# One 8 KB gather per expert slot from a side-by-side U and V table, and a weighted sum through diagonals

## What is computed

```python
s = jnp.einsum('thcd,ckd->thck', q, subkeys)         # q = xb @ wq
sv, si = lax.top_k(s, PEER_TOPK)
cand = sv[:, :, 0, :, None] + sv[:, :, 1, None, :]   # 16 x 16 sums
top_v, top_pos = lax.top_k(cand, PEER_TOPK)
eidx = jnp.take_along_axis(cidx, top_pos, axis=-1)
g = jax.nn.softmax(top_v)
u = u_tab[eidx]
a = jax.nn.gelu(jnp.einsum('td,thkd->thk', xb, u))
v = v_tab[eidx]
return jnp.einsum('thk,thkd->td', g * a, v)
```

## Time and profile before

| | us |
|---|---|
| median of 3 runs | 4904.78 (4903.73 to 4910.56) |
| the profiled execution, its own time | 4917.18 |
| the profiled execution, its span | 4915.5 |
| first gather of PEER issued at | 1783.13 |
| busy in the span: PE, DVE, POOL, ACT | 3810.6, 2952.9, 2278.9, 437.3 |
| moved by DMA | 1213.27 MB, of which 1124.21 MB by POOL's queue |

### The profile page before, as it was taken

How to read it: one execution, slowest core, us unless ns; L and a number is a source line. 1 busy time by engine, 2 the same in 40 slices (tenths; PEclk the granted TensorE clock), 3 DMA queues, 4 the chain that set the end, 5 groups by cost and what they waited for, 6 DMA issues and landing times.

```text
span 4915.5 us, 38276 instructions
## 1 busy us (share of the span) xinstructions
PE 3810.6 (78%) x11459; PEld 1541.3 (31%) x11459; DVE 2952.9 (60%) x7681; ACT 437.3 (9%) x1045; POOL 2278.9 (46%) x2121
## 2 busy tenths in 40 slices
PE   5699899899999853157777777767777777777789
PEld 3355355355445432112222222222222222211122
DVE  4466656646656658866666666656666656666620
ACT  2112112112212200000000000000000000000000
POOL 0000000000000014567767767767767767777765
PEclk7799999999989976589999999999989999999999
DMA  4210410410410146789999999999999999999999
GB/s 149 56 44 19 125 38 25 124 37 20 129 37 19 44 173 205 244 299 372 383 350 380 386 340 380 379 340 384 378 347 386 374 344 374 375 365 376 377 351 344
DMA packets 387569, 1213.27 MB, mean 247 GB/s; under 512 B 60792, under 2 KB 101296, under 8 KB 386392
## 3 DMA queue, kind: packets, MB, share of 16 engines
q0 software_dynamic: 308112, 1124.21, 61.2%
q1 hardware_dynamic: 79304, 87.29, 5.7%
HBM read 1181.66 MB, written 29.14 MB: 246 GB/s over the span
## 4 chain that ended last, share of the span: by engine, by line
POOL 23%; DMA 17%; PE 12%; issue 8%; DVE 6%; ACT 0%; SPq 0%; DVEq 0%; ACTq 0%; POOLq 0%
DMA weights<-in_peer_v,c_idxT 13%; POOL weights L1588 12%; POOL c_ub L1588 11%; PE c_acc L1710 7%; DMA c_ub<-in_peer_u,c_idx 3%; PE c_po L1636 2%; DVE c_ub L1902 2%; PE c_pq L1659 1%; DMA weights<-mixT_d 1%; PE c_acc L1700 1%; DVE c_hot L1855 0%; DVE c_hot L1851 0%; DVE c_es L1857 0%; DVE c_yt L1879 0%; PE c_po L1719 0%
## 5 line engine op out<-in xcount | busy, mean ns | idle before, releaser
L1710 PE MATMUL c_acc<-weights,c_Z 128*32 128x512 f32 x4096 | 1721.0, 602 | 532.8 <-DMA weights<-in_peer_v,c_idxT 530.5
L1902 DVE CUSTOM_DVE_ANT_0 c_ub<-c_ub,c_h 128x1024 f32<-128x1024 f32 x1024 | 1242.6, 1224 | 936.0 <-DMA c_ub<-in_peer_u,c_idx 930.5
L1588 POOL DMA_INDIRECT weights<-in_peer_v,c_idxT x1024 | 1148.8, 1122 | 413.1 <-issue 213.6
L1588 POOL DMA_INDIRECT c_ub<-in_peer_u,c_idx x1024 | 1068.6, 1044 | 509.1 <-issue 295.7
L821 PE MATMUL b_pj<-weights,b_hcB 128*128 128x512 f32 (+1 forms) x2560 | 1025.4, 558 | 1.1 <-ACT b_s_v L1049 1.1
L1710 PEld LDWEIGHTS c_acc<-weights,c_Z 128*32 128x32 f32 x4096 | 346.4, 109 | 1777.8 <-DMA weights<-in_peer_v,c_idxT 1136.7
L821 PEld LDWEIGHTS b_pj<-weights,b_hcB 128*128 128x128 f32 x2560 | 488.5, 192 | 489.1 <-issue 474.4
L482 POOL DMA_DIRECT2D weights<-in_w_in x40 | 36.0, 911 | 1113.9 <-PE b_pj L821 1091.8
L1659 PE MATMUL c_pq<-c_wq,weights 128*128 128x256 f32 (+1 forms) x1152 | 276.8, 395 | 2.3 <-ACT weights L1735 2.3
L1659 PEld LDWEIGHTS c_pq<-c_wq,weights 128*128 128x128 f32 (+1 forms) x1152 | 209.0, 186 | 81.4 <-issue 41.8
L1742 ACT ACTIVATE c_qs<-c_pq 128x256 f32<-128x256 f32 (+1 forms) x72 | 27.5, 382 | 1981.0 <-PE c_pq L1659 1981.0
(11 more groups left out here) (340 smaller groups left out, 3085.0 us busy)
## 6 DMA issues: line engine op xcount, KB each, us to landing
weights<-in_w_in POOLq DMA_DIRECT2D x32, 1024.0 KB, 8.1
b_hcB<-hT_d SPq DMA_DIRECT2D x32, 512.0 KB, 3.6
c_ub<-in_peer_u,c_idx POOLq DMA_INDIRECT x1024, 6.1
weights<-in_peer_v,c_idxT POOLq DMA_INDIRECT x1024, 6.2
b_s_C<-in_state_mlstm_c SPq DMA_DIRECT2D x8, 1024.0 KB, 12.7
out_s_c<-b_s_C SPq DMA_DIRECT2D x8, 1024.0 KB
c_wq<-in_peer_wq SPq DMA_DIRECT2D x4, 2048.0 KB, 18.7
a_x<-in_x_prompt SPq DMA_DIRECT2D x8, 512.0 KB, 4.5
```

Of the source, the lines that this page charges most:

```text
L1588: nc.gpsimd.indirect_dma_start(out=out, out_offset=None, in_=io[table], in_offset=bass.IndirectOffsetOnAxis(ap=at, axis=0)).then_inc(loade ...
L1710: last = nc.tensor.matmul(acc[half][j * SUB:(j + 1) * SUB, :], Z[:, lo:lo + SUB], vb[:, turn % RV, half * 512:(half + 1) * 512], start=Fal ...
L1902: nc.vector.tensor_tensor_reduce(ub[:, turn % RU, :], ub[:, turn % RU, :], h2[:, b, :], 1.0, 0.0, ALU.mult, ALU.add, a[:, b, k:k + 1]).the ...
```

## The change

ACT gets two DMAs at the start of the mixer, which copy `peer_u` and `peer_v` into one DRAM table `uv_d` with rows of 8 KB: U row, then V row. POOL waits for both before the first gather of PEER.

A slot has now a single item "u". POOL gathers 128 rows of `uv_d`, a token per partition (1 MB), into one of 7 buffers `rows_b`. DVE takes the dot with the U half. ACT does three instructions per slot: Gelu of the 128x1 dots, the product with the softmax share, and `diag`, the identity scaled by that weight (4 buffers). PE multiplies `diag` with the V half into `acc`, four matmul records of 128x128 by 512, and this releases the buffer. The sums of a tile live in PSUM, which has two of them now. To make room "q" writes into `po`, and there is one `psc` instead of two. `idxT`, `wT`, `fill`, `Z` and the batched "gelu" are gone; "softmax" is done head by head. The seven items of a head (q, qT, sc, best, sums, pick, softmax) stand at seven slots in a row. Heads start every 7 slots for tile 0 and every 9 for tile 1 (both during tile 0), every 14 for tiles 2 to 7, every 10 for the sample tile.

```diff
@@ mixer, ACT's stream
+            for table, at in (("peer_u", 0), ("peer_v", D)):
+                act.dma_start(res["uv_d"][:, at:at + D], io[table]).then_inc(res["table_built"], 16)
...
@@ peer_schedule
+    def head(n, hd):
+        return [(what, n, hd) for what in ("q", "qT", "sc", "best", "sums", "pick", "softmax")]
...
+        if n == 0:
+            for hd in range(1, PH):
+                put(1 + 7 * (hd - 1), head(0, hd))
+        first, each = (50, 9) if n == 0 else (8, 14) if n + 1 < CHUNKS else (3, 10)
+        m = n + 1
+        put(first, [("out", m, 0)])
+        put(first + 1, [("out", m, 1), ("norm2", m, 0)])
+        put(first + 3, [("hT", m, 0)])
+        if n:
+            put(4, [("squares", n - 1, 0), ("final", n - 1, 0)])
+        put(first + 5, [("start", m, 0)])
+        for hd in range(PH):
+            put(first + 4 + each * hd, head(m, hd))
+        if m == CHUNKS:
             for h in range(PH):
...
+                put(108 + 2 * h, [("us", m, h)])
+            put(126, [("squares", m, 0), ("final", m, 0)])
...
@@ POOL
+            pool.wait_ge(res["table_built"], 32)
...
+                after(pool, row_used, turn - RB + 1)
+                nc.gpsimd.indirect_dma_start(out=rows_b[turn % RB], out_offset=None, in_=res["uv_d"],
+                                             in_offset=bass.IndirectOffsetOnAxis(ap=at, axis=0))\
+                    .then_inc(row_loaded[turn % RB], 16)
...
@@ PE
+                elif what in ("u", "us"):
+                    turn, final = turns[n, k], k == (SLOTS if what == "u" else PH) - 1
+                    pe.wait_ge(diag_done, turn + 1)
                     for half in range(2):
...
+                        last = nc.tensor.matmul(acc[b][half][0:rows, :], diag[:, turn % RD, 0:rows],
+                                                rows_b[turn % RB][:, D + half * 512:D + (half + 1) * 512],
+                                                start=False, stop=final)
+                    last.then_inc(row_used, 1)
...
@@ ACT
+                    act.wait_ge(idx_done, hh + 1)
+                    nc.scalar.activation(tvm[0:rows, k], tvm[0:rows, k], ACT.Exp).then_inc(exp_done, 1)
+                elif what in ("u", "us"):
...
+                    act.wait_ge(dot_done, turn + 1)
+                    nc.scalar.activation(gelu, dot, ACT.Gelu).then_inc(gelu_done, 1)
...
+                    act.wait_ge(gelu_done, turn + 1)
+                    nc.scalar.activation(weight, gelu, ACT.Copy, scale=share).then_inc(w_done, 1)
+                    act.wait_ge(w_done, turn + 1)
+                    after(act, row_used, turn - RD + 1)
+                    nc.scalar.activation(spread, ones, ACT.Copy, scale=weight).then_inc(diag_done, 1)
...
@@ DVE
+                dve.wait_ge(exp_done, n * PH + hd + 1)
```

More of the change, by code:

```diff
@@ L1341, in peer_schedule @@
 def peer_schedule():
[L1343 to L1355, removed]
-        extra = {}
[L1357 to L1365, removed]
-            for h in range(PH):
[L1367 to L1372, removed]
+    def head(n, hd):
+        return [(what, n, hd) for what in ("q", "qT", "sc", "best", "sums", "pick", "softmax")]
@@ new lines, in peer_schedule, with put @@
+    order = [("out", 0, 0), ("out", 0, 1), ("keysT", 0, 0), ("norm2", 0, 0), ("hT", 0, 0), ("start", 0, 0)]
+    order += head(0, 0)
+    for n in range(CHUNKS):
+        extra = {}
+        def put(at, items):
+            for step, item in enumerate(items):
+                extra.setdefault(at + step, []).append(item)
+        if n == 0:
[12 more added lines that the diff above has]
+        if m == CHUNKS:
+            for h in range(PH):
+                put(108 + 2 * h, [("us", m, h)])
+            put(126, [("squares", m, 0), ("final", m, 0)])
@@ L1373, in peer_schedule @@
         for o in range(SLOTS):
             order += extra.get(o, [])
[L1375 to L1379, removed]
-        lead = [("u", i + 2, k) for k in range(V_LAG)] if i + 2 < CHUNKS else [None] * V_LAG
-        if i + 1 < CHUNKS:
-            order += [("gelu", i + 1, 0), lead[0], ("weigh", i + 1, 0), lead[1], ("wT", i + 1, 0)]
@@ L1383, in peer_schedule @@
-        if i >= 0:
-            order += [("squares", i, 0)]
-        order += [lead[2]]
-        if i >= 0:
-            order += [("final", i, 0)]
-        if i + 1 < CHUNKS:
-            order += [("fill", i + 1, 0), ("start", i + 1, 0), lead[3]]
-    return [item for item in order if item is not None]
+            order.append(("u", n, o))
+    order += [("squares", CHUNKS - 1, 0), ("final", CHUNKS - 1, 0)]
+    return order
 def peer(nc, io, res):
@@ L1771, in _ @@
                     last.then_inc(squares_done, 1)
-                elif what == "gelu_s":
-                    heads = slice(k * PH // 2, (k + 1) * PH // 2)
-                    act.wait_ge(u_used, u_turn[n, (k + 1) * PH // 2 - 1] + 1)
-                    nc.scalar.activation(a_r[:, heads], a_r[:, heads], ACT.Gelu).then_inc(gelu_s_done, 1)
         @block.vector
```

243 lines of the change are left out of this document (79 added, 164 removed).

## The result

| | before | after |
|---|---|---|
| median of 4 runs | 4906.48 us (4903.73 to 4910.56) | 5530.76 us (5519.84 to 5535.15) |
| ratio, 95% interval | | 1.1268 (1.1249 to 1.1288) |
| profiled execution, span | | 5532.12 us, 5529.4 us |
| first gather of PEER | 1783.13 us | 1997.72 us |
| gathers' part | 3132 us | 3531.7 us |

The change makes the kernel 624 us slower by the medians. The two profiled executions are 614 us apart (that of before took 10.7 us more than the median of its runs): 214.6 us are lost ahead of the first gather, 399 us behind it. The first look goes to the page's slices, as in the earlier trace rows.

The account below looks back on a forecast made before the run. PEER was taken to be limited by DMA, the mixer not. To the median of 4904.8 us came +591 for ACT held behind the copy and +413 for the gathers' part: about 5910 us, range 5280 to 6480.

Parts of the forecast that it names:

- step 3: Chain of a PEER slot (gather, dot, ACT, matmuls): each part under 2.46 us, so DMA sets the pace without other work.
- step 4: Head items in PEER run through the slot chain: seven slots take 31.8 us, a head every 14 slots 44.3 us.
- a bound of +284 us: PEER's head cycles with PE at a lower granted clock, 0.84: 4.4 us more in each of 64, 284 us in all.
- step 6: Sum of the gathers' part, from PEER's first gather to the end: 3545 us, +413 against 3132.
- step 2: PEER's gather in 8 KB pieces, same 1.05 MB per slot: 2.46 us of DMA at 426 GB/s.
- The bound of no gain: PEER's gather no faster in 8 KB pieces than in 4 KB ones: 2.75 us per slot.
- step 1: Table copy at the mixer's start takes 630 us and holds ACT for 0.94 of it, +591 us; SP's loads counted 0.
- the signs that the prediction gave of being wrong: ACT starting at 180 us, DVE's idle time before dots ending with gathers, or the copy far from 213 GB/s.
- The copy not holding ACT: Rival for the mixer's start: a DMA of any size counts as one command, ACT stays free; 5318 us, 17%.
- a held ACT and a fast copy: Rival for the mixer's start: the copy takes 315 us and holds ACT 295 us; 5613 us, 5%.
- Heads that hide in the buffers: Rival: ACT is free and PEER's row buffers cover the head items, gathers at DMA's pace, -578 us; 4327 us, 7%.
- A slow copy: Rival for the mixer's start: copy at half the rate, 1260 us, ACT held 1181 us; 6499 us, 13%.

Follow-up runs that it names:

- experiment 4: Changed kernel with PE taking a slot's diagonal matmuls two slots later in its order, nothing else changed: 4962.60 us, ratio 1.01 to the kernel before.
- experiment 6: Changed kernel with only the items of a head further apart and ACT's Exp one slot ahead of softmax: 5217.69 us, ratio 1.0633 to the kernel before.
- experiment 5: Changed kernel without ACT's Gelu, weight and diagonal and PE's sum over V rows, so the dot frees the buffer: 4670.25 us (one run).
- experiment 2: Changed kernel with the copy still on ACT at the mixer's start, but in eight DMAs instead of two: 5662.59 us, ratio 1.153 to the kernel before.
- experiment 3: Changed kernel with ACT's copy in eight DMAs, two in the middle of each mixer head: 5316.44 us, ratio 1.083 to the kernel before.
- experiment 1: Changed kernel with the copy issued by POOL instead of ACT, in quarters around the mixer's heads: 5587.65 us, ratio 1.1368 to the kernel before.
- the best version: Changed kernel with copy parts in the middle of heads, PE two slots behind and head items spread: 4596.61 us, ratio 0.9369 to the kernel before.

## Why the prediction was right, and where it was not

- **The bound before, and that it would be lost** (steps 3 and 4): right. PE waits for `c_diag`, DVE for `c_psc`, POOL for PE. Experiments 4 and 6 only moved items, and gained 568 and 313 us, so the order that the chain imposes is shown as the cause. Part of the gain may be PE's clock, which rose with both.
- **The head cycle** (step 4): 44.3 us predicted, 44.2 measured. DVE's maximum came 11.2 us after "q" began instead of 12.1, and 12.9 where "start" stood between, with 1.88 us. That the sum is right to 0.1 us is in part luck. In tile 0, where the heads follow one another every seven slots, a head takes 30.4 us (ACT's copies at 2168.34 and 2198.78) and not 31.8. If it takes as much in the middle tiles, the seven slots behind it take 13.8 us and not 12.5; PE runs the first of them at a lower clock (5.40 us for eight records instead of 3.60). The lower clock stood in the prediction as a bound of +284 us; the gathers' part shows 0.91, not the 0.84 of that bound. The page of the Trainium skill ("ScalarE: Activation LUTs", section "What ACT_TABLE_LOAD costs"), by whose 2.66 us a head would have been 1.38 us longer, doesn't agree here: the Exp starts 1.29 us after the start of the load before it (3078.96 and 3080.25).
- **The gathers' part** (step 6): 3545 predicted, 3531.7 measured; a middle tile 420, and 419.9 measured. The heads of tile 0 were shorter than predicted (15 of them, by about 1.4 us each, 21 us in all), so some 8 us elsewhere were longer.
- **The gather** (step 2): 2.46 us predicted from the load of `c_wq`, 2.5 measured in experiment 5, at 422 GB/s against 426. The bound of no gain is out.
- **The held time** (step 1): this is the term that failed, and nearly all of the 379 us between forecast and result. It was put at 591 us, as 0.94 of a copy of 630 us. Measured are 220 us, as 0.49 of a copy of 454 us. Of the signs that the prediction gave of being wrong, the one on the copy came true: 295 GB/s is far from 213; and ACT started at 400, not near 770 us. Both factors were too large. The rate: the memory moved 2 x 295 = 590 GB/s counting reads and writes, so the 426 GB/s of a load into SBUF is no ceiling for both together, nor is the copy as fast as if only one side counted (315 us); 454 lies between the bounds. The hold: the reading of the earlier trace rows, some 128 pieces per DMA engine, is wrong. What holds the issuer is the DMA ahead of it on its queue (experiments 2 and 3). With 0.49 and 454 us in place of the two factors the sum is 4904.8 + 220 + 413 = 5538, 7 us above the result. That the forecast's range held the result owes something to its width, 1200 us for rival values of this very term. The rule of the Trainium skill that the prediction named ("Perfetto Trace Analysis", section "DMA Instruction — HWDGE (DVE, Sync)"), that the generator is locked until all descriptors are made, agrees only in part: the first issue, of 67 MB, took 0.63 us, and the second 219.94.
- **SP's loads** (step 1, counted 0, up to 30): right in the sum only because ACT was held in the same time. The loads did suffer, taps landing in 27.3 us, and DVE stood until 318.88. With ACT free and a part of the copy at the start of each head, the first gather came 281 us late, more than with the hold, and the waits that show are those for SP's late DMAs (experiment 1).
- **The rivals.** The copy not holding ACT, 5318 us, is what experiment 3 then gave with 5316. The prediction treated the hold as a property of the chip, either there or not; it can be chosen, by where the second issue stands. The case nearest to the result, a held ACT and a fast copy (5613 us, 5%), is not what happened: its copy took 315 us and its hold 295. Heads that hide in the buffers (4327) were not seen, and with the gathers and dots alone the end would be at 1783 + 2666 = 4449, so that its 578 us were put too high as well. A slow copy didn't show. Of the figures of the Trainium skill that the prediction named ("DMA: Bandwidth & Descriptors", section "Latency and other measured facts"), both the 103 GB/s for rows 4 or 8 MiB apart and the 207 to 214 lie below the 295 of this copy. In experiment 3 quarters of one table took 67.5 and 63.4 us, 249 and 265 GB/s, beside the mixer's other loads.

What stays open: the 141 us between the best version and the gathers and dots alone, which hold PE's waits for diagonals (244.4 and 165.2 us by the groups) and the once-per-tile items; no run takes them apart. Open too is how much of the gains in experiments 4 and 6 is PE's clock, and what more row buffers or diagonals would give, since no run changes their number.

## What to carry to other kernels

When two streams become one chain, write down for each engine what stands ahead of the chain's next link in program order: here the sum over one slot stood between the steps of a head, and moving it two slots back on one engine gave back 568 us without a byte less. Look at the clock as well when such waits are cut: PE did the same work in 2407 us instead of 2638 when its waits were spread. On ACT's queue a large DMA was cheap to issue with nothing ahead of it (0.54 to 0.71 us), and with another ahead it held ACT for nearly all of what was left of that one: space such issues out. Where the copy ran beside the small loads and stores at the start of a head, it cost 110 us at the first head and 54 to 61 at each of the others; in the middle of the heads it cost nothing that shows.
